# Norm rows written whole on VectorE, and the residual scale moved out of the rows

## What is computed

```python
def layer_norm(x, g, b):
    mu = jnp.mean(xf, -1, keepdims=True)
    var = jnp.mean(jnp.square(xf - mu), -1, keepdims=True)
    return (xf - mu) * lax.rsqrt(var + LN_EPS) * g + b

for i in range(DEPTH):                                   # DEPTH = 2
    mix = conformer_conv(x, ...) if i == 0 else windowed_gqa(x, ...)
    x = layer_norm(DEEPNORM_ALPHA * x + mix, ln_mix_g[i], ln_mix_b[i])
    f = conv_ffn(x, ffn_w_up[i], ffn_w_dw[i], ffn_b_dw[i], ffn_w_down[i])
    x = layer_norm(DEEPNORM_ALPHA * x + f, ln_ffn_g[i], ln_ffn_b[i])

def conv_ffn(x, w_up, w_dw, b_dw, w_down):
    g, u = jnp.split(depthwise_conv(x @ w_up, w_dw, b_dw), 2, axis=-1)
    return (jax.nn.silu(g) * u) @ w_down
```

## Time and profile before

| | us |
|---|---|
| median of 3 runs | 3066.86 (3065.12 to 3067.67) |
| profiled execution, its own time | 3065.41 |
| its span, first to last instruction | 3063.5 |
| TensorE busy | 2896.8, 95% |
| VectorE busy | 1693.3, 55% |
| ScalarE busy | 810.2, 26% |
| GpSimd busy | 983.9, 32% |
| mean granted clock of TensorE | 0.975 |

### The profile page before, as it was taken

One profiled execution on the slowest core, in us unless ns is written; L12 is line 12 of the kernel. 1 busy time (PEld: TensorE's weight loads), 2 busy tenths in 40 slices (PEclk: granted clock), 3 DMA queues, 4 the chain that ended last, 5 costly groups with the idle time before them and its releaser, 6 DMA issues.

```text
span 3063.5 us, 36286 instructions
## 1 busy us (share of the span) xinstructions
PE 2896.8 (95%) x14070; PEld 2358.9 (77%) x14070; DVE 1693.3 (55%) x2622; ACT 810.2 (26%) x1903; POOL 983.9 (32%) x817
## 2 busy tenths in 40 slices
PE   8999959889999999999899899898899999999996
PEld 7888847778888888888688544577788888888884
DVE  3689963774444444444720698656744444444457
ACT  2212343421111111222321466504211111111221
POOL 3354402262332233223131333323522332233323
PEclk9999979999999999999899899999999999999998
DMA  3000003111111111111121000211111111111111
GB/s 129 28 22 19 28 1 117 28 32 38 42 42 32 38 42 42 35 42 36 61 69 31 21 1 1 77 51 28 42 35 35 42 42 35 35 42 42 38 36 71
DMA packets 156952, 124.71 MB, mean 41 GB/s; under 512 B 27953, under 2 KB 133849, under 8 KB 156792
## 3 DMA queue, kind: packets, MB, share of 16 engines
q1 hardware_dynamic: 149736, 96.85, 10.8%
q10 hardware_dynamic: 7056, 25.69, 2.2%
HBM read 112.03 MB, written 10.49 MB: 40 GB/s over the span
## 4 chain that ended last, share of the span: by engine, by line
PE 85%; DVE 9%; ACT 4%; issue 1%; DMA 0%; POOL 0%; POOLq 0%; DVEq 0%; SPq 0%; ACTq 0%
PE bank L631 26%; PE bank L636 26%; PE bank L634 26%; PE bank L988 3%; PE bank L964 2%; DVE conv_acc L1360 2%; PE bank L979 1%; DVE stats L1290 1%; ACT y L1145 1%; ACT gained_tile L1033 1%; PE bank L663 1%; ACT probs L1240 1%; DVE y L1580 1%; DVE y L1307 0%; DVE y L1309 0%
## 5 line engine op out<-in xcount | busy, mean ns | idle before, releaser
L631 PE MATMUL bank<-x_hi,w_hi 128*128 128x512 f32 (+1 forms) x2688 | 958.3, 357 | 47.5 <-DVE up_conv L1488 25.0
L634 PE MATMUL bank<-x_lo,w_hi 128*128 128x512 f32 (+1 forms) x2688 | 953.7, 355 | 0.0
L636 PE MATMUL bank<-x_hi,w_lo 128*128 128x512 f32 (+1 forms) x2688 | 953.7, 355 | 0.0
L544 POOL CAST w_hi<-raw_pieces 128x512 fp32r<-128x512 f32 x348 | 340.6, 979 | 1740.0 <-issue 1240.0
L631 PEld LDWEIGHTS bank<-x_hi,w_hi 128*128 128x128 f32 x2688 | 510.2, 190 | 124.9 <-issue 39.7
L634 PEld LDWEIGHTS bank<-x_lo,w_hi 128*128 128x128 f32 x2688 | 510.1, 190 | 70.7
L636 PEld LDWEIGHTS bank<-x_hi,w_lo 128*128 128x128 f32 x2688 | 509.6, 190 | 71.1
L548 POOL TENSOR_TENSOR w_lo<-raw_pieces,w_hi 128x512 fp32r<-128x512 f32 x348 | 481.0, 1382 | 27.9
L1521 DVE TENSOR_TENSOR y<-y,bank 128x512 f32<-128x512 f32 x440 | 296.2, 683 | 211.8 <-PE bank L636 206.7
L1482 DVE SCALAR_TENSOR_TENSOR gate_conv<-bank,ffn_conv_table,gate_conv 128x510 f32<-128x510 f32 x132 | 86.2, 653 | 349.9 <-ACT up_conv L1177 347.9
L1360 DVE SCALAR_TENSOR_TENSOR conv_acc<-glu,conv_table,conv_acc 128x1024 f32<-128x1024 f32 (+1 forms) x310 | 257.6, 908 | 35.4 <-ACT conv_acc L1085 35.4
(11 more groups left out here) (152 smaller groups left out, 3945.8 us busy)
## 6 DMA issues: line engine op xcount, KB each, us to landing
raw_pieces<-in_ffn_w_up_dram SPq DMA_DIRECT2D x168, 256.0 KB, 2.9
raw_pieces<-in_ffn_w_down_dram SPq DMA_DIRECT2D x84, 256.0 KB, 2.6
raw_pieces<-in_conv_w_pw_dram SPq DMA_DIRECT2D x48, 256.0 KB, 2.7
y<-in_x_prompt_dram ACTq DMA_DIRECT2D x16, 512.0 KB, 6.5
residual_dram<-y ACTq DMA_DIRECT2D x10, 512.0 KB, 2.7
y<-residual_dram ACTq DMA_DIRECT2D x10, 512.0 KB, 9.9
out_dram<-y SPq DMA_DIRECT2D x10, 512.0 KB, 2.6
raw_pieces<-in_attn_w_q_dram SPq DMA_DIRECT2D x32, 128.0 KB, 2.4
```

What stands on the lines that cost most here:

```text
L544: pool.tensor_copy(WH[:, p % RING, :], raw[:, p % RAW, :]).then_inc(piece_hi, 1)
L631: mm = pe.matmul(out, left[0], right[0], start=first, stop=False)
L634: pe.matmul(out, left[0], right[1], start=False, stop=False)
L636: return pe.matmul(out, left[1], right[0], start=False, stop=last)
```

## The change

The norm writes the whole row. `norm_apply` becomes two SCALAR_TENSOR_TENSOR operations of VectorE, (x - mean)·gain and then ·rstd + shift, so y holds x itself. `keep_tile` and its buffers go: ScalarE casts the turned bank straight to XH (`x_high`, two operations a tile) and VectorE subtracts the bank and XH for XL (`x_low`, two operations a tile). A bank is free for the next turn when the low part is made (`turned_lo`), not when ScalarE has read it. `scale_gains`, `residual_tile` and `pool_residual` go with all their waits. Because x is added unscaled, what is added to it is divided by ALPHA: in the FFN's product, in the copy of v, and the epsilon of norms 1 to 3 by ALPHA squared; a layer norm gives the same for a row and its multiple. The gain and shift rows of norm 1 are loaded into the place of XH and XL of tile 9, after the last up-chunk of the FFN. The lists keep their order, with "split" named "low" and "gain" named "high".

```diff
-    pe.wait_ge(ln_ready, TT * (use - 1) + t + 1)
-    if before:
-        pe.wait_ge(gained, TT * (use - 1) + before[-1] + 1)
-for half in range(2):
-    if use == 0 and before:
-        pe.wait_ge(turned_lo, 2 * before[-1] + half + 1)
+    pe.wait_ge(ln_ready, TT * (use - 1) + t + 1)
+for half in range(2):
+    if before:
+        pe.wait_ge(turned_lo, 2 * (TT * use + before[-1]) + half + 1)
...
-if k == 0 and n == 1 and t == 8:
-    pe.wait_ge(gained, TT * norm + 1)
+if k == 0 and n == 1 and t >= 8:
+    pe.wait_ge(turned_lo, 2 * TT * (norm + 1) + t - 7)
...
 def norm_apply(ln, t):
-    dve.tensor_scalar(y[:, t, :], y[:, t, :], mv[:, t, 0:1], rstd[:, t:t + 1], ALU.subtract,
-                      ALU.mult).then_inc(ln_ready, 1)
+    dve.wait_ge(gains_landed, GAINS_BY[ln])
+    dve.scalar_tensor_tensor(out=tile, in0=tile, scalar=mv[:, t, 0:1], in1=gain_row,
+                             op0=ALU.subtract, op1=ALU.mult).then_inc(vec_step, vs.one())
+    dve.wait_ge(vec_step, vs.now())
+    dve.scalar_tensor_tensor(out=tile, in0=tile, scalar=rstd[:, t:t + 1], in1=shift_row,
+                             op0=ALU.mult, op1=ALU.add).then_inc(ln_ready, 1)
...
-    if use:
-        residual_tile(1, t)
-        dve.wait_ge(*RES_DONE(1, t))
-    else:
+    if use == 0:
...
-    if 3 * f + ch < RES_SPLIT:
-        residual_tile(use - 1, 3 * f + ch)
...
-    dve.tensor_tensor(ub, gb, ub, ALU.mult).then_inc(ffn_prod, 1)
+    dve.scalar_tensor_tensor(out=ub, in0=gb, scalar=1.0 / ALPHA, in1=ub, op0=ALU.mult, op1=ALU.mult
+                             ).then_inc(ffn_prod, 1)
...
-ffn_stretch(B_FFN1, B_FFN1 + 8)
-pool_residual(2)
-ffn_stretch(B_FFN1 + 8, N_PIECES)
+ffn_stretch(B_FFN1, N_PIECES)
...
-    keep(v_sb[:, j, :], KVD)
+    keep(v_sb[:, j, :], KVD, scale=1.0 / ALPHA)
```

More of the change, by code:

```diff
@@ L75, in trunk @@
     DEPTH = w["ffn_w_up"].shape[0]
-    NORMS = 2 * DEPTH - 1
     PE_TAPS = 9
@@ L123, in trunk @@
             shift_end = sb("shift_rows_end", [P, D], where=a)
+        with ExitStack() as a:
+            rows_mid = [sb(f"{name}_rows_mid", [P, KT, T], where=a) for name in ("gain", "shift")]
         XH = sb("x_hi", [P, KT, XW], F32R)
@@ L179, in trunk @@
         with ExitStack() as a:
[L180 to L184, removed]
+            sb("below_v", [P, 3 * HW + 2 * D], where=a)
             v_sb = sb("v", [P, TT, KVD], where=a)
@@ L464, in trunk @@
         GAINS_BY = [32, 64, 96, 128]
+        GAIN_ROWS = [(gain[:], shift[:]), [rows[:, :, T - P:T] for rows in rows_mid], (gain[:], shift[:]),
+                     (gain_end[:], shift_end[:])]
         TURN_BANK = [[4, 6, 4, 6, 4, 6, 4, 6, 4, 4], [0, 2, 2, 4, 6] + [4, 6, 4, 6, 4], [0] * TT,
                      [0, 2, 2, 4, 6] + [4, 6, 4, 6, 4]]
[L468 to L476, removed]
         GLU_COL = [PAD, PAD + HALF, PAD + S0 + PAD]
@@ L586, in normalise_half @@
                 ins.then_inc(probs_ready_pool, 1)
[L588 to L595, removed]
             def ffn_stretch(first, end):
@@ L1012, in load_gains @@
                 for rows, vec in zip(where, norm_vectors(ln)):
-                    act.dma_start(rows, vec.to_broadcast([P, D])).then_inc(gains_landed, 16)
-            def scale_gains(ln):
-                act.wait_ge(gains_landed, GAINS_BY[ln])
-                for rows in (gain, shift):
-                    ins = act.activation(rows[:], rows[:], ACT.Copy, scale=ALPHA)
-                ins.then_inc(gains_ready, 1)
+                    vec = vec.to_broadcast([P, D])
+                    if len(rows.shape) == 3:
+                        vec = vec.rearrange("p (k t) -> p k t", t=P)
@@ L1022, in deviation @@
+                    act.dma_start(rows, vec).then_inc(gains_landed, 16)
             def deviation(ln, t):
                 act.wait_ge(var_ready, TT * ln + t + 1)
-                act.activation(std[:, t:t + 1], mv[:, t, 1:2], ACT.Sqrt, bias=eps[:, 0:1]).then_inc(std_ready, 1)
-            def keep_tile(ln, t):
-                for half in range(2):
-                    act.wait_ge(turned, 2 * (TT * (ln + 1) + t) + half + 1)
-                    if half == 0 and t >= 2:
-                        act.wait_ge(turned_lo, 2 * (TT * (ln + 1) + t - 1))
-                    for k in range(4 * half, 4 * half + 4):
-                        ins = act.activation(SCALED_TILE[ln][t % 2][:, k, :],
-                                             bank[TURN_BANK[ln + 1][t] + half][:, cols(k % 4)],
-                                             ACT.Identity, scale=chan[:, 5 + 2 * ln, k:k + 1],
-                                             bias=chan[:, 6 + 2 * ln, k:k + 1])
-                ins.then_inc(gained, 1)
+                act.activation(std[:, t:t + 1], mv[:, t, 1:2], ACT.Sqrt, bias=eps[:, 1 if ln else 0:][:, 0:1]
+                               ).then_inc(std_ready, 1)
@@ L1220, in _ @@
                     deviation(1, j)
-                elif what == "gain":
-                    keep_tile(1, j)
+                elif what == "high":
+                    x_high(2, j)
                     act.dma_start(residual_rows[j], y[:, j, :]).then_inc(res_stored, 16)
@@ L1275, in _ @@
             vs = Count()
-            def keep_split(use, t):
-                whole = SCALED_TILE[use - 1][t % 2]
-                dve.wait_ge(gained, TT * (use - 1) + t + 1)
-                dve.tensor_copy(XH[:, :, cols(t)], whole[:]).then_inc(vec_step, vs.one())
-                dve.wait_ge(vec_step, vs.now())
-                dve.tensor_tensor(XL[:, :, cols(t)], whole[:], XH[:, :, cols(t)].bitcast(F32), ALU.subtract
-                                  ).then_inc(turned_lo, 2)
             def norm_stats(ln, t, written):
@@ L1525, in add_pair @@
                     for i in range(first, end):
-                        if g == 0 and i < TT:
-                            dve.wait_ge(*RES_DONE(use - 1, i))
                         add_down(20 * g + i, i % TT, i // TT)
```

86 lines of the change are left out of this document (30 added, 56 removed), and 6 rows, old and new, of tables (END_ORDER_V, PROJ_ORDER_V).

## The result

The kernel after takes 3034.61 us (median of 4 runs, 3032.91 to 3037.70), the kernel before beside it 3066.45: a ratio of 0.9897 with a 95% interval of 0.9880 to 0.9915. That is 31.8 us faster. 3045.5 had been predicted, with a range that ended at 3035.0: the median lies 0.4 us outside it, less than the four runs differ among themselves, and 10.9 under the forecast.

A forecast was written before the change was run, and what follows sets the result against it. TensorE was taken as the bound nearly everywhere, so only its waits counted. C -8.9, B +5.7, A and D -9.1 each sum to -21.4 on the profiled 3065.41, 3044.0; plus 1.45 for the median, 3045.5, range 3035 to 3060.

The forecast's parts named there:

- Edits with no price: Across the kernel: product's new form, v scaled in its copy, 1/ALPHA in epsilon, fewer small loads; claimed to cost nothing.
- C: Start of the attention's output projection: adds no longer queue behind VectorE's residual operations, -8.9 us.
- B: Norm 1 at the end of FFN 0: turns wait for late low parts instead of ScalarE's bank read, +5.7 us.
- the walk: Operation-by-operation timing at the end of FFN 0, from norm 0's reciprocal: k 0.0 begins 8.5 us later.
- A: Norm 0 into FFN 0: the big wait before chunk 3's taps goes, a new 6.9 wait at turn 6 comes; -9.1 us.
- beside weight splits I take 1.75 each: New norm's two VectorE halves beside weight splits: 1.75 us per half, between 1.28 and 2.20.
- rival 3: Norm halves block at the port shared with GpSimd, 3.37 us each beside a split: slower, 3073 us; chance 0.04.
- D: Norm 2 into FFN 1: claimed to repeat the gain at norm 0 into FFN 0, -9.1 us.
- six small loads fewer: Kernel start: loads removed with no price, since VectorE's table copy there isn't on a wait of TensorE.
- Rival 2: Lower costs: end of FFN 0 +2, both FFN starts -12 each, output projection unchanged; -31, 3036 us; chance 0.13.

The follow-up runs named there:

- e2: Kernel after with unused bytes ahead of the same buffers, so that all lie exactly where they lay in the kernel before: 3042.35 us, ratio to before 0.9920.
- e4: Kernel after with the FFN product as a plain TENSOR_TENSOR again, its division by ALPHA left out (other output): 3036.1 us.
- e3: Kernel after with VectorE's low parts moved up around all three norms, norm 1's turns 0 to 3 on two bank pairs, downs between: 3013.5 us, ratio 0.9833.
- f4: Kernel after with tiles 1 and 3 of norm 1 turned into banks 2 and 3 instead of 0 and 1, orders unchanged: 3030.8 us.
- f1: Kernel before with one unused tensor that moves h up by 128 bytes, otherwise untouched: 3052.95 us, ratio 0.9955.
- g1: Kernel after with 64 unused bytes ahead of all buffers, the weights too: 3034.7 us.
- g2: Kernel after with 128 unused bytes ahead of all buffers, the weights too: 3033.8 us.

## Why the prediction was wrong

Its mechanisms held, place by place, and its sum was short by what it did not list. The step that failed is the one that put "Edits with no price" at nothing.

- **C, -8.9:** measured -9.2; the wait was 0.26, "under 1 us".
- **B, +5.7:** k 0.0 came 8.5 later against the reciprocal of norm 0 (32.8 instead of 24.2), the 8.5 of the walk. Turn 1 waited 12.9 where some 13 were named. v 0 came 5.7 later, the sum 6.4 less 0.7. Behind v 0 another 1.2 came back, which the walk did not follow. The rows of norm 1, for which it allowed up to 30 us, landed in 4.0 and 5.3.
- **A, -9.1:** -8.7. Turn 6 itself came where the walk had it, 42.4 behind turn 0, but its wait was 4.72 and not 6.9: the walk let TensorE reach it 7.7 behind the start of the first up-projection, while it takes 9.8 in before and after alike, at a mean granted clock of 0.81 and 0.83. Chunk 1 was 4.6 late and not 5.1, chunk 3 earlier by 6.7 and not 7.0, and 2.0 of half clock came back behind it, for the 2.1. The step "beside weight splits I take 1.75 each" was a little high: the eight halves of norms 4 to 7 took 1.6 in the mean. Timelines of VectorE, then of GpSimd, after:

```profile
577.22 1.30 DVE L1240 SCALAR_TENSOR_TENSOR y<-y,mean_var,gain_rows 128x1024 f32<-128x1024 f32 x1
578.55 2.18 DVE L1243 SCALAR_TENSOR_TENSOR y<-y,rstd,shift_rows 128x1024 f32<-128x1024 f32 x1
...
583.62 1.94 DVE L1240 SCALAR_TENSOR_TENSOR y<-y,mean_var,gain_rows 128x1024 f32<-128x1024 f32 x1
585.59 1.29 DVE L1243 SCALAR_TENSOR_TENSOR y<-y,rstd,shift_rows 128x1024 f32<-128x1024 f32 x1
```

```profile
577.51 2.13 POOL L529 TENSOR_TENSOR w_lo<-raw_pieces,w_hi 128x512 fp32r<-128x512 f32 x1
```

  Of the 60 halves of norms 0 to 2, nine took 1.51 to 2.42, all beside a weight split, and the others 1.29. GpSimd's subtraction, begun 0.3 behind the start of a half, stretches from 1.29 to 2.13, and the next half, begun 1.1 ahead of the subtraction's end, to 2.18: each is longer by a little less than the other had left. So rival 3 had its mechanism and not its size: a half met only the rest of a subtraction of 1.29, which cost 1.1 at most, and the rival needs 3 us a half.
- **D, "the same" as A:** it gained 1.4 more than the sum. From turn 0 to chunk 3, D takes 81.3 before and 72.1 after, A 80.2 and 73.5; taking D as A was not exact in either kernel. The clock is most of it: chunk 1 with its two turns takes 12.8 in A and 14.4 in D before (mean granted clock 1.00 and 0.88), and 14.2 in A and 12.8 in D after (0.89 and 1.00), each time behind a wait of 2.6 to 2.8. Why the clock fell in one and not in the other stays open.
- **"Edits with no price":** the failed step. It listed "six small loads fewer" and did not ask what the smaller tables do: they moved h by 192 bytes, from distance 128 to 192 from the weights, and that is 7.7 us by the medians (e2 against after), seven tenths of the miss of 10.9, and 9.2 by the two profiled executions (3039.6 and 3030.4). The product itself did cost nothing (e4). Most of the rest of the miss is D and B, 1.4 and 1.2, within the walks' own bounds.
- **Rival 2, 3036,** is within 1.4 us of the measured time, and that is luck. It had B at +2 and A and D at -12 each; they came to +4.5, -8.7 and -10.5, and 7.7 us came from a cause that it did not have.

With h held in place the kernel after takes 3042.35, inside the range and 3.2 under the forecast. The range was too narrow since all its cases were of one kind, waits and their handovers, and none allowed a matmul to take another time. That the median fell 0.4 us outside it and not just inside is chance; the missing 7.7 is not.

## What to carry to other kernels

Removing an operation takes its buffers with it: compare the table of memory locations before and after, and hold the place of what TensorE reads, or the run tests two changes. Where back-to-back matmuls are over 0.227 us apart for 512 columns at full clock and nothing is waited for, try an unused tensor ahead of the stationary operand, so that it starts at the same place modulo 256 bytes as the moving one. When a bank's release moves from one engine to another, move the releasing step in that engine's order with it: with the second pair of banks and TensorE's turns moved to match, that was worth 21 us here (e3), as much as the predicted gain of the change. The banks alone gave 1.9 in B (f4).

## What the runs showed of the hardware

Matmuls of 512 fp32r columns with a weight load each follow each other at 0.2269 us when both operands start at the same place modulo 256 bytes, and at 0.2289 to 0.2343 at other distances (27.23 to 28.11 for 120). In before the pattern is regular: a gap of 0.240 or 0.241 at every seventh matmul. It is the same in e2, another program with h at the same place, and lacking in f1, where all gaps but the first five are 0.226 or 0.227. The products of x and the weights have distance 0 in every run and a median gap of 0.226; moving both together (g1, g2) did not change them. The taps of the convolution, whose distance changes in steps of 4 bytes, lie between 0.225 and 0.234. The Trainium skill, "SBUF — State Buffer", Who interferes with whom, gives TensorE one read port for the moving operand and one for the weight load and calls them independent. By that one would not expect the distance to matter, and the measurement speaks against it, at least as far as their places go. Why the distance counts, and whether the period is the same for other sizes and types, no run here shows.
